# A fused three-block layer stack on one core: state-space heads with rounded row sums, mask in PSUM and biased exponentials

## The reference

```
acum   = cumsum(a)                                  # over the 256 tokens
lmat   = exp(acum[t] - acum[s]) for s <= t, else 0
y_diag = sum_s (C[t] . B[s]) * lmat[t, s] * (x[s] * dt[s])
y      = y_diag + d_skip * x
y      = rms_norm over 256 columns of (y * silu(z)), times a gain
```

## Time and profile before

| | us |
|---|---|
| median of 3 runs | 3162.65 |
| lowest, highest | 3162.60, 3168.82 |
| the profiled execution | 3157.97 |
| its span (first to last instruction) | 3156.2 |
| TensorE busy | 3008.6 (95%) |
| VectorE busy | 2012.5 (64%) |
| ScalarE busy | 1357.1 (43%) |
| GpSimd busy | 182.8 (6%) |

### The profile page before, as it was taken

One profiled execution on the slowest core, in us unless ns is written; L12 is line 12 of the kernel. 1 busy time (PEld: TensorE's weight loads), 2 busy tenths in 40 slices (PEclk: granted clock), 3 DMA queues, 4 the chain that ended last, 5 costly groups with the idle time before them and its releaser, 6 DMA issues.

```text
span 3156.2 us, 52697 instructions
## 1 busy us (share of the span) xinstructions
PE 3008.6 (95%) x19072; PEld 2674.2 (85%) x19072; DVE 2012.5 (64%) x3581; ACT 1357.1 (43%) x1983; POOL 182.8 (6%) x196
## 2 busy tenths in 40 slices
PE   8999899998999999999999999998998899999998
PEld 8987777897999699898799776987798888888887
DVE  5565644656556655656755664797599866766665
ACT  4443513344345344434344553654446734443433
POOL 0000000000000000000000000000057700000000
PEclk9999999999999999999999999999999999999999
DMA  7564353555555455555365543532443255555554
GB/s 262 187 203 138 102 178 128 173 186 199 187 186 174 170 188 183 185 186 175 129 203 186 190 154 116 169 113 94 147 155 100 63 185 187 187 185 181 178 181 144
DMA packets 140271, 523.73 MB, mean 166 GB/s; under 512 B 15650, under 2 KB 15650, under 8 KB 137312
## 3 DMA queue, kind: packets, MB, share of 16 engines
q1 hardware_dynamic: 134768, 490.79, 47.1%
q0 software_dynamic: 4784, 29.94, 2.5%
q10 hardware_dynamic: 576, 1.05, 0.1%
HBM read 520.65 MB, written 1.06 MB: 165 GB/s over the span
## 4 chain that ended last, share of the span: by engine, by line
PE 75%; DVE 10%; ACT 3%; issue 2%; DMA 0%; ACTq 0%; DVEq 0%; SPq 0%
PE psum L506 69%; PE psum L1733 2%; DVE wpair L477 1%; PE psum L1917 1%; ACT wpair L474 1%; PE psum L655 1%; PE psum L1718 1%; ACT arena L1295 0%; DVE small L2978 0%; PE psum L1278 0%; DVE arena L2957 0%; DVE st L1325 0%; PE psum L1254 0%; DVE xpair L718 0%; DVE arena L2868 0%
## 5 line engine op out<-in xcount | busy, mean ns | idle before, releaser
L477 DVE TENSOR_TENSOR wpair<-ring,wpair 128x1024 fp32r<-128x1024 f32 (+1 forms) x862 | 1044.5, 1220 | 745.7 <-ACT wpair L474 741.8
L506 PE MATMUL psum<-xpair,wpair 128*128 128x256 f32 x11712 | 1475.6, 285 | 22.5 <-DVE wpair L477 12.3
L506 PEld LDWEIGHTS psum<-xpair,wpair 128*128 128x128 f32 x11712 | 1444.6, 193 | 59.6 <-DVE wpair L477 32.5
L474 ACT CAST wpair<-ring 128x1024 fp32r<-128x1024 f32 (+1 forms) x888 | 918.9, 1044 | 822.4 <-PE psum L506 767.7
L506 PE MATMUL psum<-wpair,hpair 128*128 128x512 f32 x3120 | 753.4, 392 | 7.7 <-DVE hpair L930 7.7
L506 PEld LDWEIGHTS psum<-wpair,hpair 128*128 128x128 f32 x3120 | 573.7, 189 | 120.9 <-issue 10.7
L506 PE MATMUL psum<-wpair,xpair 128*128 128x512 f32 (+3 forms) x1728 | 407.1, 395 | 7.6 <-DVE xpair L718 2.5
L506 PEld LDWEIGHTS psum<-wpair,xpair 128*128 128x128 f32 x1728 | 326.3, 195 | 77.4 <-issue 8.5
L905 ACT ACTIVATE small<-psum 128x256 f32<-128x256 f32 x132 | 50.7, 384 | 232.8 <-PE psum L506 232.8
L941 ACT ACTIVATE small<-psum 128x256 f32<-128x256 f32 x92 | 35.4, 384 | 262.2 <-PE psum L506 262.2
L919 DVE TENSOR_TENSOR small<-small,psum 128x256 f32<-128x256 f32 x132 | 55.5, 421 | 137.8 <-ACT small L905 137.8
(11 more groups left out here) (324 smaller groups left out, 1808.3 us busy)
## 6 DMA issues: line engine op xcount, KB each, us to landing
ring<-wstream SPq DMA_DIRECT2D x934, 512.0 KB, 3.3
arena<-rows POOLq DMA_DIRECT2D x18, 1024.0 KB, 5.4
arena<-diag POOLq DMA_DIRECT2D x2, 1728.0 KB, 10.3
arena<-tbuf POOLq DMA_DIRECT2D x2, 1024.0 KB, 7.3
arena<-x_feat ACTq DMA_DIRECT2D x4, 256.0 KB, 7.4
res<-x_tok POOLq DMA_DIRECT2D x1, 1024.0 KB, 7.0
arena<-mem_feat POOLq DMA_DIRECT2D x1, 1024.0 KB, 4.9
arena<-keys POOLq DMA_DIRECT2D x1, 1024.0 KB, 7.6
```

The source lines that it names most:

```text
L474: eng.copy(hi, raw).then_inc(S("w_hi"), 1)
L477: eng.tensor_tensor(wpair[:, 1, o % PAIRS, 0:w], raw, hi.bitcast(F32), ALU.subtract)\
L506: mm = pe.matmul(out_, a[i], b[j], start=start and n == 0, stop=stop_ and last)
```

## The change

- The row sums of all heads are computed once, transposed: two products put acum of the 64 rows (32 heads, twice) into PSUM bank 5. VectorE turns them into `segs` in the rounded type: rows 0 to 31 the rounded sum, rows 32 to 63 what rounding left. In the loop one product of 64 rows and 384 columns, with a column of ones and zeros (`pick_row`) spread over all rows, gives acum[t] of a head; a second one adds a mask of -1e30 above the diagonal to two blocks of 128 columns (identity by `after_ut`).
- ScalarE takes the exponential straight from PSUM, with -acum[s] as a bias column: two instructions a head. VectorE's two subtractions and its masking of C.B are gone.
- VectorE multiplies by C.B in PSUM, in place in ebuf (now 4 buffers; mbuf is gone): one instruction of 128x384. The factor dt goes into xs: GpSimd multiplies it in, 8 products of 128x512, each behind its skip term.
- The sigmoids of block 0 of gssd move behind the loop; the casts and subtractions of slots 4 and 5 move to heads 6 and 7 in it.
- GpSimd makes the constants in hpair, which is free there.

```
-        cbt = region(16448, 2, 384)
-        ebuf = region(17216, 2, 384)
-        mbuf = region(17984, 2, 384)
+        flat_h = hpair[:, :, :, :].rearrange("p a b s -> p (a b s)")
+        segs, after_ut, ident_r, pick_row = (flat_h[0:64, 0:384], flat_h[:, 384:512], flat_h[:, 512:640],
+                                             flat_h[0:64, 640:672])
+        ebuf = region(17216, 4, 384)
@@ GpSimd, behind load_row("norm2")
+            pool.tensor_scalar(after_ut, ut, 1.0, -NEG, ALU.subtract, ALU.mult)
+            pool.tensor_copy(ident_r, ident)
+            pool.tensor_tensor(pick_row, ident[0:64, 0:32], ident[0:64, 32:64], ALU.add).then_inc(S("ssd_consts"), 1)
+            pool.wait_ge(S("steps"), 1)
+            for m in range(4):
+                for t in range(NT):
+                    pool.wait_ge(S("skip3"), NT * m + t + 1)
+                    xm = xs[:, t, m * HALF:(m + 1) * HALF].rearrange("p (h d) -> p h d", d=64)
+                    dt = tiny[:, 9, 32 * t + 8 * m:32 * t + 8 * m + 8]
+                    pool.tensor_tensor(xm, xm, dt.unsqueeze(2).to_broadcast([P, 8, 64]), ALU.mult)\
+                        .then_inc(S("x_steps"), 1)
@@ TensorE
-            pe.matmul(psum[:, 4, 32:64], ut, a_tok[:, 32:64], start=False, stop=True).then_inc(S("acum"), 1)
+            pe.matmul(psum[:, 4, 32:64], ut, a_tok[:, 32:64], start=False, stop=True)
+            pe.matmul(psum[0:64, 5, 0:256], tiny[:, 0, :], uto[:, 0:256], start=True, stop=False)
+            pe.matmul(psum[0:64, 5, P:256], tiny[:, 2, :], ut, start=False, stop=True).then_inc(S("acum"), 1)
             pe_tok(pe, "gssd", xt, (0,))
-            pe.wait_ge(S("acum_out"), 1)
+            pe.wait_ge(S("segs"), 1)
+            pe.wait_ge(S("ssd_consts"), 1)
...
-                            pe.wait_ge(S("cb_out"), g - 1)
+                            pe.wait_ge(S("mready"), 4 * (g - 1))
...
-                        pe.wait_ge(S("seg"), i - 1)
+                        pe.wait_ge(S("sexp"), i - 1)
                     b = psum[:, 4 + i % 2, :]
-                    pe.matmul(b[:, 0:256], a_tok[:, i:i + 1].to_broadcast([P, P]), uto[:, 0:256], start=True, stop=False)
-                    pe.matmul(b[:, P:256], a_tok[:, 32 + i:33 + i].to_broadcast([P, P]), ut, start=False,
-                              stop=True).then_inc(S("rowsum"), 1)
+                    pe.matmul(b[:, 0:384], pick_row[:, i:i + 1].to_broadcast([64, P]), segs, start=True, stop=False)
+                    pe.matmul(b.rearrange("p (c s) -> p c s", s=P)[:, 0:3:2, :], ident_r,
+                              after_ut.unsqueeze(1).to_broadcast([P, 2, P]), start=False, stop=True)\
+                      .then_inc(S("rowsum"), 1)
                 h = i - 2
                 if h >= 0:
-                    g, m = h // 4, mbuf[:, h % 2, :]
+                    g, m = h // 4, ebuf[:, h % 4, :]
+                    if h % 8 == 0:
+                        pe.wait_ge(S("x_steps"), NT * (h // 8 + 1))
                     pe.wait_ge(S("mready"), h + 1)
@@ ScalarE
-            gates("gssd", (0,))
+            split.cover("gssd", 0, more=0)
...
+            act.wait_ge(S("segs"), 1)
             for h in range(SSD_H):
-                act.wait_ge(S("seg"), h + 1)
-                act.activation(ebuf[:, h % 2, :], ebuf[:, h % 2, :], ACT.Exp).then_inc(S("sexp"), 1)
+                act.wait_ge(S("rowsum"), h + 1)
+                if h >= 4:
+                    act.wait_ge(S("ydone"), h - 3)
+                b = psum[:, 4 + h % 2, :]
+                act.activation(ebuf[:, h % 4, 0:256], b[:, 0:256], ACT.Exp, bias=tiny[:, 12, h:h + 1])
+                act.activation(ebuf[:, h % 4, 256:384], b[:, 256:384], ACT.Exp, bias=tiny[:, 12, 32 + h:33 + h])\
+                   .then_inc(S("sexp"), 1)
+                if h in (6, 7):
+                    split.step()
                 if h >= 10 and h % 4 in (2, 3):
                     squares((h - 10) // 4, h % 4 - 2)
...
-            gates("gssd", (1,))
+            gates("gssd")
@@ VectorE
+                chain.mark(dve.scalar_tensor_tensor(
+                    out=T(2 * t).rearrange("p (a h) -> p a h", a=2), in0=T(9)[:, c].unsqueeze(1).to_broadcast([P, 2, 32]),
+                    scalar=-1.0, in1=T(11)[:, 0:32].unsqueeze(1).to_broadcast([P, 2, 32]), op0=ALU.mult, op1=ALU.mult))
...
             dve.wait_ge(S("acum"), 1)
-            copy(T(12), psum[:, 4, 0:64]).then_inc(S("acum_out"), 1)
-            dve.wait_ge(S("acum_out"), 1)
-            split.cover("gssd", 0)
+            chain.mark(dve.tensor_scalar(T(12), psum[:, 4, 0:64], -1.0, None, ALU.mult))
+            chain(copy(segs[:, 0:256], psum[0:64, 5, 0:256]))
+            chain(dve.tensor_tensor(segs[32:64, 0:256], psum[32:64, 5, 0:256], segs[32:64, 0:256].bitcast(F32),
+                                    ALU.subtract))
+            copy(segs[:, 256:384], segs[:, P:256].bitcast(F32)).then_inc(S("segs"), 1)
+            split.cover("gssd", 0, more=0)
...
-            for i in range(SSD_H + 7):
+            for i in range(SSD_H + 5):
                 if i < SSD_H:
...
-                    dve.wait_ge(S("rowsum"), i + 1)
-                    b, e = psum[:, 4 + i % 2, :], ebuf[:, i % 2, :]
-                    chain.mark(dve.tensor_scalar(e[:, 0:256], b[:, 0:256], T(12)[:, i:i + 1], 0.0, ALU.subtract, ALU.min))
-                    dve.tensor_scalar(e[:, 256:384], b[:, P:256], T(12)[:, 32 + i:33 + i], 0.0, ALU.subtract,
-                                      ALU.min).then_inc(S("seg"), 1)
...
+                    h, g = i, i // 4
                     dve.wait_ge(S("sexp"), h + 1)
+                    dve.wait_ge(S("cb_done"), g + 1)
+                    e = ebuf[:, h % 4, :]
+                    dve.tensor_tensor(e, e, psum[:, 6 + g % 2, 0:384], ALU.mult).then_inc(S("mready"), 1)
+                    if h in (6, 7):
+                        split.step()
-                h = i - 4
+                h = i - 3
                 if h >= 0 and h % 4 == 3:
```

More of the change, by code:

```diff
@@ L2733, in skip_term @@
                 for t in range(NT):
[L2734 to L2737, removed]
+                    dve.tensor_tensor(y3[:, t, c].rearrange("p (h d) -> p h d", d=64),
+                                      xs[:, t, c].rearrange("p (h d) -> p h d", d=64),
+                                      hrow[:, 192 + 8 * m:200 + 8 * m].unsqueeze(2).to_broadcast([P, 8, 64]),
+                                      ALU.mult).then_inc(S("skip3"), 1)
             s = STAGES["xbc"]
@@ L2773, in _ @@
             dve.wait_ge(S("c_uto"), 16)
-            for i in range(SSD_H + 7):
+            dve.wait_ge(S("skip3"), 8)
+            for i in range(SSD_H + 5):
                 if i < SSD_H:
[L2776 to L2780, removed]
-                    dve.wait_ge(S("rowsum"), i + 1)
-                    b, e = psum[:, 4 + i % 2, :], ebuf[:, i % 2, :]
-                    chain.mark(dve.tensor_scalar(e[:, 0:256], b[:, 0:256], T(12)[:, i:i + 1], 0.0, ALU.subtract, ALU.min))
-                    dve.tensor_scalar(e[:, 256:384], b[:, P:256], T(12)[:, 32 + i:33 + i], 0.0, ALU.subtract,
-                                      ALU.min).then_inc(S("seg"), 1)
-                h = i - 1
-                if 0 <= h < SSD_H:
-                    g = h // 4
-                    dve.wait_ge(S("sexp"), h + 1)
-                    dve.wait_ge(S("cb_out"), g + 1)
-                    if h >= 2:
-                        dve.wait_ge(S("ydone"), h - 1)
-                    m, e, c = mbuf[:, h % 2, :], ebuf[:, h % 2, :], cbt[:, g % 2, :]
-                    chain.mark(dve.scalar_tensor_tensor(out=m[:, 0:256], in0=e[:, 0:256], scalar=T(9)[:, h:h + 1],
-                                                        in1=c[:, 0:256], op0=ALU.mult, op1=ALU.mult))
-                    dve.scalar_tensor_tensor(out=m[:, 256:384], in0=e[:, 256:384], scalar=T(9)[:, 32 + h:33 + h],
-                                             in1=c[:, 256:384], op0=ALU.mult, op1=ALU.mult).then_inc(S("mready"), 1)
-                    dve.wait_ge(S("mready"), h + 1)
-                h = i - 4
+                    h, g = i, i // 4
+                    dve.wait_ge(S("sexp"), h + 1)
+                    dve.wait_ge(S("cb_done"), g + 1)
[4 more added lines that the diff above has]
+                h = i - 3
                 if h >= 0 and h % 4 == 3:
@@ L2805, in _ @@
                        .then_inc(S("yout"), 1)
-                h = i - 6
+                h = i - 5
                 if h >= 0 and h % 4 == 3:
```

## The result

The changed kernel takes **3186.68 us** (median of 4 runs, 3185.4 to 3193.91), the kernel before 3164.72 (4 runs, one more than in the table above): a ratio of 1.0076, 95% interval 1.0059 to 1.0093. I had forecast 3142, so the sign was wrong: slower by 0.76% where 0.65% faster was expected. Of the rivals, the one on the slow side (TensorE's clock falls in the loop, 3176, chance 0.05) is what happened, and it cost more than I had priced.

A forecast was written before the change was run, and what follows sets the result against it. VectorE was taken to bound the loop at 1.80 us a head, TensorE after the change. Loop end 2159.15 to 2138.0 gains 21.1, less 0.3 behind it: 3162.65 - 20.8 = 3141.8, forecast 3142, range 3134 to 3153.

The forecast's parts named there:

- rival 3: Head loop: TensorE's clock falls to 0.50, the loop's 34.1 us become 68.2, 3176 us; chance 0.05 with other mishaps.
- TensorE's load, row sum: Head loop: row sum as two rounded products, 384 and 256 columns, 0.29 us a head together (bounds 0.24 and 0.65).
- y products: Head loop, TensorE: a head's y products cost 0.66 us, unchanged, of a new load of 1.11 us.
- ScalarE's pair: Head loop: two exponentials from PSUM with a bias column, 0.76 us a pair (bounds 0.69 and 0.86).
- VectorE's product: Head loop: one 128x384 product a head with an operand in PSUM, 0.551 us like L2779.
- rival 2: Head loop: the latency loop binds, a head takes 1.4 us, 9.3 us more, 3151; chance 0.16 together with rival 4.
- The stall for the splits at heads 6 and 7: Head loop: VectorE's in-order queue delays the products of heads 7 and 8; stall 2.8 us (bounds 0 and 4.5).
- The sum: Whole kernel: 21.1 us gained up to the loop's end less 0.3 behind it, 20.8 us, giving 3142.
- Start: Ahead of the loop: group product at 2098.48, first y product at 2101.14 instead of 2102.56; no sigmoid or table-load wait.
- rival 1: Ahead of the loop: GpSimd's eight products hold VectorE up, up to 5.9 us in place of 1.0, 3147; chance 0.15.
- Behind the loop: After the loop: sigmoids and table load delay ScalarE's cast, 0.3 us later, passed on to VectorE's split and the end.
- rival 4: Head loop: VectorE stays the bound or row sum costs 0.65, 1.47 us a head, 3153; chance 0.16 with rival 2.

The follow-up runs named there:

- e1: The changed kernel with one spare single-column exponential ahead of ScalarE's wait for segs, so its table loads early: 3186.62 us against 3161.61 before, ratio 1.0077.
- e2: The changed kernel with the row-sum product over 128 rows instead of 64, the added rows zeros: 3146.03 us, ratio 0.9948 to the kernel before.
- e9: e2 with TensorE's products of a head also waiting for VectorE's product of the next head, a hole in every head: 3157.45 us, ratio 0.9976.
- e5: The kernel before with its first row-sum product (256 columns, fp32) reading 64 rows instead of 128: 3207.11 us against 3164.73, ratio 1.0126.
- e7: The changed kernel with the row-sum product over 96 rows, rows 64 to 95 zeros: median 3147.05 us, one of five runs 3168.34; ratio 0.9937.
- e10: e2 with the exponential's table loaded early as in e1: 3143.59 us against 3166.39 for the kernel before, ratio 0.9927.
- e8: e2 with GpSimd's eight products held back until the convolution of the last tile is done: 3145.51 us, ratio 0.9928 to the kernel before.
- e6: The changed kernel without the 64-row product, mask product over all 384 columns, bias zero, decay left out: 3143.54 us, ratio 0.9937 to the kernel before.
- e11: e10 with GpSimd's eight products held back until the convolution is done, as in e8: 3144.34 us, ratio 0.9938 to the kernel before.
- e12: e10 with one group product computed twice more at the loop's start, to fill TensorE's wait: 3145.24 us, ratio 0.9932 to the kernel before.

## Why the prediction was wrong

**The step that failed: rival 3 was dismissed by an argument that its row does not carry.** The prediction named the mechanism (rounded and 64-row products, a hole, half clock) and put against it that "the clock is 1.00 in the loop with more holes than it will have". That row bears on holes, and there it holds: e1, e2 and e9 show that the clock falls without the hole, comes back behind it when the rows are full, and isn't kept down by 12% idle time. It says nothing on 64-row products, of which the loop of before had none. With the earlier trace rows taken as evidence on the one and silence on the other, the chance should have been far more than 0.05. What the runs showed in its place: with a 64-row row sum in every head the clock falls to 0.50 and stays there for 78 us, and the loop takes 84.5 us for 39.5. e2 (zeros added, clock back), e5 (64 rows put into the old loop, clock gone) and e7 (96 rows: half clock in one run of five) show it from three sides. The price "34.1 us become 68.2" was short too: the loop took 84.5, and the late weight loads at half clock (32 x 0.49 = 15.7) are nearly all of the difference.

The trace of before had rows with 64 of them in use, in an attention stage that I didn't look at. Its windows, all engines first and then L1254 alone (PE and PEld), its larger group, and a weight load behind such a product:

```profile
1870.00:1940.00 70.00, 68.91 (x356) 55.53 (x355) 40.61 (x87) 34.28 (x92) 0.00 (x0) 1.00 0.32 101
1870.00:1940.00 70.00, 13.51 (x59) 8.90 (x60) 1.00 0.32 101
L1254 PE MATMUL psum<-arena 64*128 64x256 f32 x31 | 8.8, 403 | 0.0
1920.81 2.61 PEld L506 LDWEIGHTS psum<-wpair,xpair 128*128 128x128 f32 x12 [0.33 <-issue]
```

The late load is there, 0.33 us, and would have warned that the row sum can cost more than its columns. But the clock is at 1.00, with 64-row products in 13.5 of 68.9 busy us (20%; in the changed loop L1834 is 13.0 of 52, 25%). They come there in short groups between long runs of full-row products of 512 columns. So 64 rows alone don't lower the clock everywhere: in this loop and in e5, where such a product comes in every head, they do.

**TensorE's load, row sum (mis-sized too).** 0.29 us a head at full clock, "bounds 0.24, if a 64-row weight load hides, and 0.65". The pair took 0.68: above the upper bound, since the weight loads on both sides of the 64-row product did not run beside matmuls, which I had priced only as something to gain. With 128 rows the pair takes 2131.20 - 2130.82 = 0.38; the 384 columns 0.26 and the mask 0.12 for my 0.17 and 0.12. The y products took 2131.78 - 2131.20 = 0.58 for 0.66, so a head 0.96 for 0.95: two misses that cancel.

**What was right, once the rows are full.** TensorE is the bound (7.00 of 7.00 busy in e10, VectorE 5.38, ScalarE 5.67). ScalarE's pair: rows of the kernel after, group, 2085 to 2205 us, are 0.473 and 0.361 for the forecast 0.470 and 0.394; VectorE's product 0.554 for 0.551, though that was a guess from L2779.

```profile
L2813 DVE TENSOR_TENSOR arena<-arena,psum 128x384 f32<-128x384 f32 x32 | 17.6, 554 | 55.4 <-ACT arena L2179 55.4
L2178 ACT ACTIVATE arena<-psum,arena 128x256 f32<-128x256 f32 x32 | 15.1, 473 | 49.1 <-PE psum L1835 49.1
L2179 ACT ACTIVATE arena<-psum,arena 128x128 f32<-128x128 f32 x32 | 11.5, 361 | 0.0
```

From first group product to first y product 2.66 were forecast and 2.87 measured in e10; the loop from 2098.48 to 2138.0, 39.5 us, and measured 2105.12 to 2144.67, 39.6. The latency of rival 2 does not bind. The stall for the splits at heads 6 and 7 is there (TensorE busy 4.04 of 5 us at 2115 to 2120, VectorE 5.00), but it is 1.6 us, not 2.8: two row sums stand 1.77 and 1.61 us apart in place of 0.96, the next 0.2 more. The last four heads, from their group product on, took 0.7 us more than I had added up, the other groups 0.3 together, and the start 0.2. So the 39.6 is in part luck: a stall priced 1.2 too high hid small misses the other way. The sum, 20.8 us to gain, is what e10 gains: 23 us by the medians (0.9927 of 3166, interval 19 to 28), 20 (19.7) from row to row of the profiles. It needed two edits that are not in the change.

**Start.** The table load that I had taken as gone "under cover" came behind ScalarE's wait, on the path: 1.3 us from group product to first y product (4.15 in e2, 2.87 in e10). In the changed kernel, e1 shows, it is worth nothing beside the clock. The other 1.7 us by which e2's loop is longer than e10's (42.5 for 39.6) are its dip, 0.66 over 5 us.

**GpSimd (rival 1).** Forecast 1.0 of bounds 0 to 5.9, measured 2.2. I took the direction from one row, in which GpSimd waits; e8 shows that VectorE waits as well, 3.1 us over the stage. The Trainium skill (SBUF — State Buffer, "Who interferes with whom") says that the two exclude each other in whichever order they come; the trace agrees now for both directions, with 8 x 0.7 = 5.6 us lost on GpSimd and 3.1 on VectorE. The four long products fit it: each starts while GpSimd's second product of a pair is under way, ends about 0.28 us behind it and takes 0.78 more than the others. The row that I had read shows the case the other way round, GpSimd waiting for a split of VectorE's.

**Behind the loop.** The forecast of 0.3 us more was measured as 0.2 (21.35 and 21.58 us): the wait at L1864 grew from 5.64 to 6.29, and the products ahead of it ran faster (13.46 us for 13.91), which paid for most of it.

**What stays open.** Rows in use, and the weight load that doesn't overlap, always came together at 64 rows; at 96 rows the load overlaps and the clock was low in one run of five. So, as far as one run shows, fewer rows can hold the clock down without a late load; what of them TensorE's clock answers to was not taken apart, nor why the attention stage of before, with 20% of 64-row products, keeps 1.00. Nor is it known why e2, e6, e8 and e9 dip to half clock for a few microseconds at the start of the loop, e11 behind the splits, and e10 and e12 not at all. A dip costs 1.7 us in e2 and e11. That it comes back with full rows and not with 64 is what the runs show.

## What to carry to other kernels

Where a product with few rows in use goes into a dense stretch of TensorE, look for rows of that same height, placed as densely, and where there are none keep the half clock as a rival with a real chance. Filling up the rows is cheap to try: here zeros in the unused 64 rows, which cost two memsets, made the difference between 0.8% slower and 0.5% faster. When a change makes TensorE the bound, its clock in that stretch is the first term of the sum; ask for each row that speaks for 1.00 whether the products behind it are of the kind that is coming. And an argument that answers one half of a rival leaves the other half at its full chance.

## What was unexpected of the hardware

- With 64-row row sums among its products TensorE stayed at a granted clock of 0.50 from 2112 us to the end of the loop at 2191 while it was busy 7.00 of 7.00 us; with full rows it stood at 1.00 while busy 8.82 of 10.00 (e9). In another stage of the kernel before 64-row products left it at 1.00.
- Behind a 64-row product the weight load of the next one comes late by 0.3 us at half clock (32 of 32 times), and a pair takes 0.68 us at full clock against 0.38 with 128 rows. With 96 rows there is no gap (one profile).
- ScalarE's table load was not done ahead of the waits in front of its exponential: it began after 3.72 us in an idle queue, and a spare exponential ahead of them (e1) moved it off the path.
- Four of VectorE's 96 products with two SBUF inputs took 1.26 us in place of 0.48 while GpSimd multiplied beside them, the others nothing more, and GpSimd's took 1.71 us in place of 1.01.
